# Sample attention of a hybrid decoder step on Trainium2: two samples over two GLU units, in one PSUM bank

## The chip, the cores and the metric
One core of a Trainium2 chip (trn2) runs the program. The metric is the device time of one execution in microseconds (us); of several runs the median counts. Engines are called PE (TensorE, the matmuls), DVE (VectorE), ACT (ScalarE), POOL (GpSimd) and SP (SyncE, which issues most transfers).

## The reference, cut to what matters
One layer of a decoder serves 256 prompt tokens and 8 samples of 4 new tokens each (288 tokens in all). Each token gets 16 query heads on 4 key/value heads of 64 features. A sample token attends over its sample's 256 cached positions (two pages of 128, found through a page table) and the 4 new ones; the indexer's choice of keys enters as a mask.

```python
def _dsa_block(q, qi, wi, qpos, k, v, ki, kpos):
    ...
    s = jnp.einsum('btngd,btjnd->btngj', qg, k_g) * (D_HEAD ** -0.5)
    s = jnp.where(valid[:, :, None, None, :], s, -jnp.inf)
    p = jax.nn.softmax(s, axis=-1)
    o = jnp.einsum('btngj,btjnd->btngd', p, v_g)
    return o.reshape(b, t, ATTN_W).astype(q.dtype)
...
    y_a = attn @ w_attn_proj
    z = jax.nn.gelu(s5_y).astype(x.dtype)
    glu_a, glu_g = jnp.split(z @ w_glu, 2, axis=-1)
    y_b = glu_a * jax.nn.sigmoid(glu_g)
    merged = jax.nn.sigmoid(ga) * y_a + jax.nn.sigmoid(gb) * y_b
    x = x + merged @ w_out
```

## The kernel before, in words
The kernel runs the layer as a stream of weight chunks. A chunk is 4 k-tiles x 256 columns (128x1024 values, one of 4 slots). SP loads it into raw, ACT rounds it to whi (`hi`, L861 to 868), DVE makes the rest wlo = raw - whi (`lo`, L1215 to 1220), and PE multiplies it in `group` (L511 to 533): three matmuls per k-tile and column tile, L528, L529, L530, with 288 tokens moving. Each engine runs its own list of instructions in order; semaphores join them. The stages follow each other: input projections, 8 gate units with the S5 scan, 8 GLU units (`N_GLU`), 4 projection units, w_out, w_up, w_down.

The change is in the 8 GLU units, 0 to 7. Each has two groups of two chunks (the gate columns into banks 2 and 3 of acc, then the value columns into banks 0 and 1), 96 big matmuls in all. The attention is laid between them: unit i does pair of prompt heads i and sample i.

- **PE** (L680 to 779). `unit_head`, before the first group: prompt values of unit i-1 (L724), prompt scores of unit i (L687), transposes of the sample's probabilities (L538 on psb). `unit_middle`, before the second group: sample values (L739 on the two pages, L741 on the four new keys), prompt transposes (L538 on ps), scores of sample i+1 (L696). Unit 0 is irregular: the scores of sample 0 are in its head, its transposes in the middle, and its values and the scores of sample 1 ahead of the second chunk of the second group (`first_samples`).
- The scores of one sample: for each pair p of key/value heads, qbs (128 feature rows of two heads x 32 columns, 16 per head, zeros for the other head) are the weights and the 260 keys move; the output is 32 partitions x 260 in bank 3 of aux. The values: vpg (128 positions x 64 features) are the weights, and 16 columns of probabilities pTb move; the output is already turned (features on partitions), in bank 0 of aux. A matmul of fp32 operands shows as two records.
- **DVE** (L1525 to 1600) masks and takes the maximum, scales psb by the reciprocal of the sum before it is transposed, and makes att_lo. **ACT** (L1048 to 1115) does the exponentials, the copies to pTs and pTb, att_hi, and the Sigmoid of the gate half (L1112), which frees the gate banks for the next unit. The exponential and the Sigmoid need different function tables; each switch loads one.
- **POOL** (L1950 to 2015) copies queries and new keys into qs, ks, qbs and kTb with a multiplication by `half` (1 for one half of the rows and 0 for the other) or by ones, then starts the transfers of the gates (gbt, ga) and multiplies yb. **SP** (L441 to 474) loads the next chunk of w_glu, the pages of the sample (`pages_in`) and its mask in between.
- Early in the program DVE builds small constants (`constants`, L1307 to 1317) after its tiles of the keys' chunks; the next thing that it does is the wlo of the values' first chunk (L1220). POOL fills `half` (L1763 to 1765) at its start, ahead of the S5 angles (L1768, L1771), whose sine ACT takes at L954 and L955.

Of the kernel before, what the change touches and what calls it, by code (L numbers as in the profile page):

```python
# [108 lines left out]
def hybrid_decoder_step_kernel(nc, I, O, W):  # L109
# [72 lines left out]
    half = at("half", [P, 2], F32, GR + 36832)  # L182
# [40 lines left out]
    qbs = at("qbs", [P, NPR, 32], F32, WK + 43168)  # L223
    psb = at("psb", [64, SK], F32, WK + 16160)
    pTb = at("pTb", [P, 3, 64], F32, WK + 17216)
    smax = at("smax", [64, 8], F32, WK + 18016)
# [6 lines left out]
    spare = at("spare", [P, 8], F32, WK + 43424)  # L233
    maskb = [at(f"maskb{i}", [64, SK], F32, GR + 10240 + 1056 * i) for i in range(2)]
# [26 lines left out]
    with ExitStack() as ctx:  # L261
# [22 lines left out]
        def sample_half(n):  # L284

            return aux[DH * n:DH * (n + 1), 0, 3 * P:3 * P + 64].rearrange("p (a n g t) -> p a n g t", a=2, n=2, g=4)[:, :, n, :, :]

        def sample_cols(tile, rows, b):

            return tile[rows, :, ds(TP + DS * b, DS)].rearrange("p (a g) t -> p a g t", a=2)  # L290
# [27 lines left out]
        def _(sp):  # L318
# [122 lines left out]
            def pages_in(i):  # L441

                u = i % 2
                pages = [sp.value_load(ptab[0:1, NPAGES * i + g:NPAGES * i + g + 1], min_val=0, max_val=NPOOL - 1) for g in range(NPAGES)]
                sp.wait_ge(sem("unit_free"), i + 1)
                for g, page in enumerate(pages):
                    sp.dma_start(kTb[u][:, :, P * g:P * (g + 1)], I["cache_k"][ds(page, 1)].rearrange("a (p q) s -> q (a p) s", p=NPR)
                                 ).then_inc(sem(f"k_in{u}"), 16)
                sp.dma_start(vnew[u][:, :], W["v_new"][DS * i:DS * (i + 1), :]).then_inc(sem(f"v_in{u}"), 16)
                for g, page in enumerate(pages):  # L450
                    sp.dma_start(vpg[u][:, g:g + 1, :], I["cache_v"][ds(page, 1)].rearrange("a p d -> p a d")).then_inc(sem(f"v_in{u}"), 16)

            def mask_in(i):

                sp.wait_ge(sem("mask_out"), 16)
                sp.dma_start(maskb[i % 2][:, :], bc(W["mask"][DS * i:DS * (i + 1), :], 0, 16)).then_inc(sem(f"mask_in{i % 2}"), 16)

            sp.wait_ge(sem("vs_stored"), 16)
            for i in range(N_GLU):
                load("w_glu", C_GLU + 4 * i, 0, 0, D + CW * i)  # L460
                pages_in(i)
                if i:
                    mask_in(i)
                load("w_glu", C_GLU + 4 * i, 1, KCH, D + CW * i)
                for q in range(2):
                    load("w_glu", C_GLU + 4 * i, 2 + q, KCH * q, CW * i)
                if i == 0:
                    mask_in(i)
# [30 lines left out]
        def _(pe):  # L499
# [190 lines left out]
            def sample_scores(i):  # L690

                u = i % 2
                pe.wait_ge(sem(f"k_in{u}"), 32 * (i // 2) + 32)
                pe.wait_ge(sem("new_ready"), 3 * i + 3)
                for p in range(NPR):
                    mm = pe.matmul(aux[32 * p:32 * p + 32, 3, 0:SK], qbs[:, p, :], kTb[u][:, p, :], start=True, stop=True)  # L696
                mm.then_inc(sem("ss_t"), 1)
# [9 lines left out]
            def sample_probs(i):  # L707
# [19 lines left out]
            def sample_values(i):  # L727

                u = i % 2
                pe.wait_ge(sem("pTb_ready"), i + 1)  # L730
                pe.wait_ge(sem(f"v_in{u}"), 48 * (i // 2) + 48)
                for p in range(NPR):
                    for g in range(NPAGES + 1):
                        for n in range(2):
                            c = slice(P * p + DH * n, P * p + DH * (n + 1))
                            k = slice(32 * p + 16 * n, 32 * p + 16 * (n + 1))
                            o = aux[DH * n:DH * (n + 1), 0, 3 * P + 32 * p + 16 * n:3 * P + 32 * p + 16 * (n + 1)]
                            if g < NPAGES:
                                mm = pe.matmul(o, vpg[u][:, g, c], pTb[:, g, k], start=g == 0, stop=False)  # L739
                            else:  # L740
                                mm = pe.matmul(o, vnew[u][:, c], pTb[0:DS, 2, k], start=False, stop=True)  # L741
                mm.then_inc(sem("unit_free"), 1)
# [12 lines left out]

            def unit_middle(i):

                pe.wait_ge(sem("p_ready"), i + 1)
                if i:
                    sample_values(i)  # L760
                prompt_probs(i)
                if i == 0:
                    sample_probs(0)
                elif i < N_GLU - 1:
                    sample_scores(i + 1)

            def first_samples():

# [1356 lines left out]
```

## Time and profile before
| what | value |
|---|---|
| median of 3 runs | 1564.46 us (1564.35 to 1564.78) |
| the profiled execution's own time | 1563.48 us |
| its span | 1561.6 us, 34462 instructions |
| PE busy | 1548.6 us, 99% |
| DVE, ACT, POOL busy | 1034.7 (66%), 668.0 (43%), 463.5 (30%) us |
| granted PE clock | 1.0 of full speed |
| GLU stage in the trace | about 411.6 to 552 us |

The page lists busy times and idle times of every engine; idle time of an engine off the path costs nothing. The view of the chain that ended last gives pieces in order of time, each starting where the one before ended, so that their lengths add up. The timeline gives start and duration of instructions (matmuls overlap, so durations there are longer than their distance); what stands in brackets is the idle time before an instruction and what ended it.

### The profile page before, as it was taken

Reading aid. Unit: us, or ns where it says so; the run is one execution under the profiler, and the core shown is the slowest. Engines: PE = TensorE matmul, PEld = TensorE weight load, DVE = VectorE, ACT = ScalarE, POOL = GpSimd, SP = SyncE. Lnnn points to the kernel's source line nnn. Section 1 sums busy time; section 2 is a strip of 40 time slices with the busy share of each in tenths; the row PEclk is TensorE's granted clock in tenths of the full one; section 3 lists DMA queues with packets and bytes.
Section 4 is the critical chain, followed back from the end, with each engine's and each line's share of the span. In section 5 each row is a group of like instructions: output and inputs, shape, how many; then the busy total and the mean of one; then the engine's idle time right before and its main releaser. Section 6 shows DMA issues by size and latency. Waiting matters only on the chain.

```text
span 1561.6 us, 34462 instructions
## 1 busy us (share of the span) xinstructions
PE 1548.6 (99%) x12846; PEld 1529.0 (98%) x12846; DVE 1034.7 (66%) x1487; ACT 668.0 (43%) x899; POOL 463.5 (30%) x601
## 2 busy tenths in 40 slices
PE   9999999999999999999999999999999999999998
PEld 9999999999999999999999999999999999999998
DVE  7755788888566666557776777777767664444443
ACT  6334345445477644444333333333434333333332
POOL 8994467876232200221121211111111110000100
PEclk9999999999999999999999999999999999999999
DMA  8887476666666677556545454555555565555552
GB/s 268 237 180 204 144 207 188 187 194 177 213 190 186 189 178 228 168 168 205 185 148 186 149 181 154 175 159 163 161 161 163 160 216 176 173 170 174 169 180 89
DMA packets 292928, 281.17 MB, mean 180 GB/s; under 512 B 29872, under 2 KB 283568, under 8 KB 292704
## 3 DMA queue, kind: packets, MB, share of 16 engines
q1 hardware_dynamic: 277264, 255.94, 54.2%
q10 hardware_dynamic: 13568, 16.62, 3.5%
q0 software_dynamic: 2000, 7.27, 1.4%
q8 instruction: 68, 1.11, 0.3%
q14 instruction: 28, 0.23, 0.0%
HBM read 266.60 MB, written 13.16 MB: 179 GB/s over the span
## 4 chain that ended last, share of the span: by engine, by line
PE 92%; POOL 5%; issue 1%; DVE 1%; DMA 1%; ACT 0%; SPq 0%; POOLq 0%; ACTq 0%
PE banks L528 29%; PE banks L530 29%; PE banks L529 29%; POOL angle L1768 1%; POOL angle L1771 1%; PE banks L538 1%; POOL sm L1768 1%; DMA raw<-in_w_in 1%; PE banks L651 1%; PE banks L665 1%; POOL sm L1771 1%; PE banks L687 0%; PE banks L724 0%; PE banks L739 0%; POOL rdec L1771 0%
## 5 line engine op out<-in xcount | busy, mean ns | idle before, releaser
L1220 DVE TENSOR_TENSOR wlo<-raw,whi 128x1024 fp32r<-128x1024 f32 x443 | 564.9, 1289 | 279.7 <-ACT whi L868 273.5
L868 ACT ACTIVATE whi<-raw 128x1024 fp32r<-128x1024 f32 x443 | 461.6, 1050 | 544.5 <-PE banks L530 482.7
L529 PE MATMUL banks<-h_lo,whi 128*128 128x288 f32 x1408 | 415.7, 295 | 0.0
L530 PE MATMUL banks<-h_hi,wlo 128*128 128x288 f32 x1408 | 415.7, 295 | 0.0
L528 PE MATMUL banks<-h_hi,whi 128*128 128x288 f32 x1408 | 414.6, 294 | 0.0
L528 PE MATMUL banks<-hhi,whi 128*128 128x288 f32 (+1 forms) x912 | 272.2, 298 | 3.3 <-DVE wlo L1220 1.6
L529 PE MATMUL banks<-hlo,whi 128*128 128x288 f32 (+1 forms) x912 | 270.0, 296 | 0.0
L530 PE MATMUL banks<-hhi,wlo 128*128 128x288 f32 (+1 forms) x912 | 269.9, 296 | 0.0
L529 PEld LDWEIGHTS banks<-h_lo,whi 128*128 128x128 f32 x1408 | 264.6, 188 | 0.1
L530 PEld LDWEIGHTS banks<-h_hi,wlo 128*128 128x128 f32 x1408 | 264.4, 188 | 0.0
L528 PEld LDWEIGHTS banks<-h_hi,whi 128*128 128x128 f32 x1408 | 264.1, 188 | 0.1
L529 PE MATMUL banks<-a_lo,whi 128*128 128x288 f32 x704 | 208.0, 295 | 1.0 <-issue 1.0
L530 PE MATMUL banks<-a_hi,wlo 128*128 128x288 f32 x704 | 207.8, 295 | 0.0
L528 PE MATMUL banks<-a_hi,whi 128*128 128x288 f32 x704 | 207.2, 294 | 0.0
L528 PEld LDWEIGHTS banks<-hhi,whi 128*128 128x128 f32 (+1 forms) x912 | 171.4, 188 | 6.3 <-issue 2.5
L529 PEld LDWEIGHTS banks<-hlo,whi 128*128 128x128 f32 (+1 forms) x912 | 171.4, 188 | 0.1
L530 PEld LDWEIGHTS banks<-hhi,wlo 128*128 128x128 f32 (+1 forms) x912 | 171.4, 188 | 0.0
L529 PEld LDWEIGHTS banks<-a_lo,whi 128*128 128x128 f32 x704 | 132.3, 188 | 1.2 <-issue 1.2
L530 PEld LDWEIGHTS banks<-a_hi,wlo 128*128 128x128 f32 x704 | 132.2, 188 | 0.0
L528 PEld LDWEIGHTS banks<-a_hi,whi 128*128 128x128 f32 x704 | 132.1, 188 | 0.0
L2018 POOL TENSOR_TENSOR sq<-x 128x576 f32 (+1 forms) x15 | 17.2, 1147 | 352.3 <-DVE x L1706 222.0
L1742 POOL TENSOR_TENSOR up<-cstate,ones 128x16 f32<-128x16 f32 x88 | 72.5, 824 | 154.2 <-DVE wlo L1220 141.4
(332 smaller groups left out, 2208.1 us busy)
## 6 DMA issues: line engine op xcount, KB each, us to landing
raw<-in_w_up SPq DMA_DIRECT2D x352, 256.0 KB, 3.4
raw<-in_w_in SPq DMA_DIRECT2D x223, 256.0 KB, 3.4
raw<-in_w_down SPq DMA_DIRECT2D x176, 256.0 KB, 2.9
raw<-in_w_glu SPq DMA_DIRECT2D x64, 256.0 KB, 3.1
raw<-in_w_out SPq DMA_DIRECT2D x64, 256.0 KB, 3.3
raw<-in_w_attn_proj SPq DMA_DIRECT2D x32, 256.0 KB, 3.9
scratch_gates<-gt ACTq DMA_DIRECT2D x16, 288.0 KB, 3.8
gbt<-scratch_gates POOLq DMA_DIRECT2D x8, 288.0 KB, 3.3
```

The costliest lines, as they stand in the source:

```text
L528: pe.matmul(out, h, xh[:, kt, :], start=kt == 0, stop=False)
L529: pe.matmul(out, h, xl[:, kt, :], start=False, stop=False)
L530: mm = pe.matmul(out, lo, xh[:, kt, :], start=False, stop=kt == nk - 1)
L538: return pe.matmul(out, in_, ident[b:b + k, b:b + k], is_transpose=True)
L651: mm = pe.matmul(aux[r, c, NCH * i:NCH * (i + 1)], lbs[r, i, c, :], ub[r, it, i, :], start=True, stop=True)
L665: mm = pe.matmul(out, clam[jt % 2][:, i, step, b + 1, :], xs[:, step, i, :], start=step == 0, stop=False)
L868: act.activation(whi[:, s, :, 0:cols], raw[:, s, :, 0:cols], ACT.Copy).then_inc(hi_ready, 1)
L1220: dve.tensor_tensor(wlo[:, s, :, 0:cols], raw[:, s, :, 0:cols], whi[:, s, :, 0:cols], ALU.subtract).then_inc(lo_ready, 1)
L1742: return pool.tensor_tensor(out, a, one.broadcast_to(list(out.shape)), ALU.mult)
L1768: own.link(pool.tensor_scalar(out, a, s1, s2, o1, o2))
L1771: own.link(pool.tensor_tensor(out, a, b, op))
L2018: own.link(pool.tensor_tensor(buf[:, :, :], x[:, ds(tile, 2), :], x[:, ds(tile, 2), :], ALU.mult))
```

## The change
Samples are taken in pairs j (samples 2j and 2j+1) over units 2j and 2j+1. Scores of both samples in the head of the even unit: 8 matmuls over one half of the rows each (64 feature rows of one head), 32 columns of weights, 260 keys moving, output to four strips of 32 partitions of bank 3, so that the 128 rows hold 4 heads x 4 queries per head x 2 samples x 4 tokens; the columns of the other sample are zeros in qbs, and the second sample accumulates on the first. One maximum and one exponential serve 128 rows. The probabilities are transposed unscaled in the middle of the even unit (three transposes of 128 rows; in unit 0 ahead of the second chunk of the second group). In the head of the odd unit they are the weights (32 columns) and the values move (64 columns), into four strips of bank 3: 24 matmuls. DVE scales these rows and puts each sample's part in place (`sample_rows`), and PE turns the 128x128 tile o_rows once in the middle of the odd unit. Nothing of the samples is in bank 0 any more. DVE gets two small constants, e8 and of_pair; POOL loses `half` and gets one memset of qbs.

```diff
@@ SP @@
+            def keys_in(j):
+                sp.wait_ge(sem("ss_t"), j) if j else sp.wait_ge(sem("pages_free"), 1)
+                for b in range(2):
+                    for g, page in enumerate(pages(2 * j + b)):
+                        sp.dma_start(kTb[b][:, :, P * g:P * (g + 1)], I["cache_k"][ds(page, 1)]
...
+            def values_in(j):
+                if j:
+                    sp.wait_ge(sem("sv_ready"), j)
+                for b in range(2):
+                    i = 2 * j + b
+                    sp.dma_start(vnew[b][:, :], W["v_new"][DS * i:DS * (i + 1), :]).then_inc(sem("v_in"), 16)
+                    for g, page in enumerate(pages(i)):
+                        sp.dma_start(vpg[b][:, g:g + 1, :], I["cache_v"][ds(page, 1)].rearrange("a p d -> p a d")).then_inc(sem("v_in"), 16)
...
                 load("w_glu", C_GLU + 4 * i, 0, 0, D + CW * i)
-                pages_in(i)
-                if i:
-                    mask_in(i)
+                if i == 0:
+                    keys_in(0)
                 load("w_glu", C_GLU + 4 * i, 1, KCH, D + CW * i)
+                if i % 2 == 0:
+                    values_in(j)
+                elif j < 3:
+                    keys_in(j + 1)
+                    mask_in(j + 1)
@@ PE @@
+            def sample_scores(j):
+                pe.wait_ge(sem("k_in"), 64 * j + 64)
+                pe.wait_ge(sem("new_ready"), 4 * j + 4)
+                if j:
+                    pe.wait_ge(sem("atts_done"), j)
+                for b in range(2):
+                    for p in range(NPR):
+                        for n in range(2):
+                            r, h = slice(DH * n, DH * (n + 1)), 2 * p + n
+                            mm = pe.matmul(aux[32 * h:32 * h + 32, 3, 0:SK], qbs[r, p, b, :], kTb[b][r, p, :], start=b == 0, stop=b == 1)
...
-                pe.wait_ge(sem("sp_ready"), i + 1)
+                pe.wait_ge(sem("sexp_ready"), j + 1)
                 for m, n in ((0, P), (1, P), (2, DS)):
-                    t = transpose(aux[0:n, 3, 64 * m:64 * (m + 1)], psb[:, m * P:m * P + n])
+                    t = transpose(aux[0:n, 3, P * m:P * (m + 1)], psb[:, m * P:m * P + n])
...
+            def sample_values(j):
+                pe.wait_ge(sem("pTb_ready"), j + 1)
+                pe.wait_ge(sem("v_in"), 96 * j + 96)
+                for b in range(2):
                     for g in range(NPAGES + 1):
+                        for h in range(NKV):
+                            k, c = slice(32 * h, 32 * (h + 1)), slice(DH * h, DH * (h + 1))
+                            o = aux[k, 3, DH * b:DH * (b + 1)]
                             if g < NPAGES:
+                                mm = pe.matmul(o, pTb[:, g, k], vpg[b][:, g, c], start=g == 0, stop=False)
                             else:
+                                mm = pe.matmul(o, pTb[0:DS, 2, k], vnew[b][:, c], start=False, stop=True)
+                mm.then_inc(sem("sv_ready"), 1)
+            def sample_turn(j):
+                pe.wait_ge(sem("o_rows_ready"), j + 1)
+                transpose(aux[:, 3, 0:P], o_rows[:, :, :].rearrange("p a d -> p (a d)")).then_inc(sem("so_t"), 1)
             def unit_head(i):
                 if i:
                     prompt_values(i - 1)
-                    pe.wait_ge(sem("atts_done"), i)
                 prompt_scores(i)
-                if i:
-                    sample_probs(i)
+                if i % 2 == 0:
+                    sample_scores(i // 2)
                 else:
-                    sample_scores(0)
+                    sample_values(i // 2)
             def unit_middle(i):
                 pe.wait_ge(sem("p_ready"), i + 1)
-                if i:
-                    sample_values(i)
                 prompt_probs(i)
...
+                if i % 2:
+                    sample_turn(i // 2)
+                elif i:
+                    sample_probs(i // 2)
@@ ACT @@
                 hi(c, 2)
                 prompt_exp(i)
-                if i == 0:
-                    sample_exp(0)
                 hi(c, 3)
+                if i % 2 == 0:
+                    sample_exp(i // 2)
                 prompt_probs_t(i)
...
+                if i % 2:
+                    sample_out(i // 2)
+                elif i:
+                    sample_probs_t(i // 2)
                 hi(c, 4)
                 if i == 0:
-                    sample_out(0)
-                if i < N_GLU - 1:
-                    sample_exp(i + 1)
+                    sample_probs_t(0)
@@ DVE @@
                 own.link(dve.tensor_reduce(e32[:, :], ident[:, :].rearrange("p (a h) -> p h a", a=4), AX_X, ALU.add))
+                own(dve.tensor_reduce(e8[:, :], ident[:, :].rearrange("p (x y) -> p y x", y=8), AX_X, ALU.add))
                 dve.tensor_tensor(ddiag[:, :, :], bc(e32[:, :], 1, NUT), bc(nvec[:, 48:56], 2, 32), ALU.mult).then_inc(sem("ddiag_ready"), 1)
+                own.wait()
+                own(dve.tensor_reduce(of_pair[:, :], e8[:, :].rearrange("p (b t) -> p b t", b=2), AX_X, ALU.add))
...
-                dve.tensor_scalar(psb[:, :], psb[:, :], smax[:, 2:3], None, ALU.mult).then_inc(sem("sp_ready"), 1)
+                own.link(dve.tensor_scalar(smax[:, 3:5], of_pair[:, :], smax[:, 2:3], None, ALU.mult))
+            def sample_rows(j):
+                dve.wait_ge(sem("sv_ready"), j + 1)
+                own.link(dve.tensor_scalar(o_rows[:, :, :], bc(aux[:, 3, 0:DH], 1, 2), smax[:, 3:4], None, ALU.mult))
+                dve.scalar_tensor_tensor(o_rows[:, :, :], bc(aux[:, 3, DH:2 * DH], 1, 2), smax[:, 4:5], o_rows[:, :, :], ALU.mult, ALU.add
+                                         ).then_inc(sem("o_rows_ready"), 1)
...
                 prompt_scale(i)
-                if i == 0:
-                    sample_scale(0)
+                if i % 2 == 0:
+                    sample_max(i // 2)
+                else:
+                    sample_rows(i // 2)
                 lo(c, 3)
...
+                if i % 2 == 0:
+                    sample_scale(i // 2)
+                else:
+                    sample_low(i // 2)
                 lo(c, 4)
@@ POOL @@
-            own.link(pool.memset(half[:, :], 0.0))
-            for n in range(2):
-                own.link(pool.memset(half[DH * n:DH * (n + 1), n:n + 1], 1.0))
...
-                if i < N_GLU - 2:
-                    pool.wait_ge(sem("ss_t"), i + 2)
-                    stage_sample(i + 2)
+                if i % 2 == 0 and i < N_GLU - 2:
+                    pool.wait_ge(sem("ss_t"), i // 2 + 1)
+                    stage_sample(i // 2 + 1)
                 gate_branch(i)
```

## Rows read from the trace of the kernel before

**Rows 1.** The page: busy time of the engines, and the group of ACT's rounding.
```profile
PE 1548.6 (99%) x12846; PEld 1529.0 (98%) x12846; DVE 1034.7 (66%) x1487; ACT 668.0 (43%) x899; POOL 463.5 (30%) x601
...
L868 ACT ACTIVATE whi<-raw 128x1024 fp32r<-128x1024 f32 x443 | 461.6, 1050 | 544.5 <-PE banks L530 482.7
```

**Rows 2.** Waits of PE over the span (us in total, times, longest).
```profile
PE banks L724 <- ACT glu_gate L1112: 0.7, 1, 0.7
```

**Rows 3.** Chain of waits, unit 4 of the GLU stage: start us, us, what.
```profile
482.39 0.81 PE banks L724 x12
483.19 0.86 PE banks L687 x8
484.06 0.16 PE banks L538 x3
...
490.79 0.34 PE banks L739 x8
491.13 0.22 PE banks L741 x4
...
491.91 0.81 PE banks L538 x6
492.71 0.56 PE banks L696 x4
493.28 0.33 PE banks L528
```

**Rows 4.** Chain of waits, middle of unit 0 and of unit 7.
```profile
419.87 0.98 PE banks L538 x9
...
544.29 0.80 PE banks L538 x6
545.09 0.13 PE banks L528
```

**Rows 5.** Chain of waits, other stages: indexer (L627), S5 inputs (L651), output transposes.
```profile
154.61 1.01 PE banks L627 x16
...
179.31 1.15 PE banks L651 x32
...
1550.40 3.21 PE banks L538 x28
```

**Rows 6.** Timeline of PE, S5 outputs: start us, us, engine line op names shapes.
```profile
401.19 0.43 PE L665 MATMUL banks<-xs,clam 128*32 128x72 f32 x16
401.44 0.31 PE L667 MATMUL banks<-ub,tlag 128*32 128x72 f32 x8
401.56 0.43 PE L665 MATMUL banks<-xs,clam 128*32 128x72 f32 x16
```

**Rows 7.** Timeline of ACT, end of unit 0.
```profile
427.33 0.51 ACT L1078 ACTIVATE psb<-psb,smax 64x260 f32<-64x260 f32 x1 [1.54 <-DVE smax L1548]
...
427.95 1.28 ACT L1112 ACT_TABLE_LOAD   x1
429.24 0.65 ACT L1112 ACTIVATE glu_gate<-banks 128x576 f32<-128x576 f32 x1
```

**Rows 8.** Timelines of POOL, ACT, DVE and PE around the constants.
```profile
5.67 0.10 POOL L1763 MEMSET half<- 128x2 f32 x1
...
6.16 0.56 POOL L1771 TENSOR_TENSOR sm<-params 128x32 f32<-128x32 f32 x2
...
82.42 0.74 ACT L954 ACTIVATE angle<-angle 128x640 f32<-128x640 f32 x1 [5.56 <-POOL angle L1826]
...
104.69 0.37 DVE L1316 TENSOR_REDUCE e<-ident 128x32 f32<-128x128 f32 x1
...
107.62 0.37 PE L528 MATMUL banks<-hhi,whi 128*128 128x288 f32 x1 [1.55 <-DVE wlo L1220]
```

**Rows 9.** Timelines of DVE and POOL in unit 4.
```profile
489.34 0.69 DVE L1540 TENSOR_TENSOR ps<-ps,pmax 128x512 f32<-128x512 f32 x1
...
493.37 0.44 POOL L1742 TENSOR_TENSOR qbs<-qT,half 128x32 f32<-128x32 f32 x2 [6.56 <-PE banks L696]
```

More of the change, by code:

```diff
@@ L181, in hybrid_decoder_step_kernel @@
     wtok = at("wtok", [P, 2, IH], F32, GR + 36608)
-    half = at("half", [P, 2], F32, GR + 36832)
+    e8 = at("e8", [P, 8], F32, GR + 36800)
+    of_pair = at("of_pair", [P, 2], F32, GR + 36832)
     nramp = at("nramp", [P, 32], F32, GR + 36672)
@@ L222, in hybrid_decoder_step_kernel @@
     kTb = [at(f"kTb{i}", [P, NPR, SK], F32, (WK + 41088, GR)[i]) for i in range(2)]
[L223 to L226, printed above, removed]
+    qbs = at("qbs", [P, NPR, 2, 32], F32, WK + 43168)
+    psb = at("psb", [P, SK], F32, WK + 16160)
+    pTb = at("pTb", [P, 3, P], F32, WK + 17216)
+    smax = at("smax", [P, 8], F32, WK + 18752)
+    o_rows = at("o_rows", [P, 2, DH], F32, WK + 18784)
     glu_a = at("glu_a", [P, 2, T], F32, WK + 19456)
@@ L232, in hybrid_decoder_step_kernel @@
     vnew = [at(f"vnew{i}", [DS, KV], F32, GR + 8192 + 1024 * i) for i in range(2)]
-    spare = at("spare", [P, 8], F32, WK + 43424)
-    maskb = [at(f"maskb{i}", [64, SK], F32, GR + 10240 + 1056 * i) for i in range(2)]
+    spare = at("spare", [P, 8], F32, WK + 43680)
+    maskb = [at(f"maskb{i}", [P, SK], F32, GR + 10240 + 1056 * i) for i in range(2)]
     ga = at("ga", [P, KD, T], F32, GR + 12416)
@@ L439, in _ @@
                         lags_in(it)
[L441 to L451, printed above, removed]
@@ L453, in mask_in, with pages @@
-            def mask_in(i):
+            def pages(i):
+                return [sp.value_load(ptab[0:1, NPAGES * i + g:NPAGES * i + g + 1], min_val=0, max_val=NPOOL - 1) for g in range(NPAGES)]
+            def keys_in(j):
+                sp.wait_ge(sem("ss_t"), j) if j else sp.wait_ge(sem("pages_free"), 1)
+                for b in range(2):
+                    for g, page in enumerate(pages(2 * j + b)):
+                        sp.dma_start(kTb[b][:, :, P * g:P * (g + 1)], I["cache_k"][ds(page, 1)].rearrange("a (p q) s -> q (a p) s", p=NPR)
+                                     ).then_inc(sem("k_in"), 16)
@@ L467, in _ @@
                 if i == 0:
-                    mask_in(i)
+                    mask_in(0)
             with loop("SP", 0, N_PROJ) as it:
@@ L1035, in gates @@
                     act.wait_ge(sem("c_ready"), 4 * N_GATE)
-                    for k in range(2):
-                        act.activation(spare[:, k:k + 1], ident[:, 0:1], ACT.Copy).then_inc(sem("unit_free"), 1)
+                    act.activation(spare[:, 0:1], ident[:, 0:1], ACT.Copy).then_inc(sem("pages_free"), 1)
                 hi(c, 6)
@@ L1972, in _ @@
                     stage_prompt(0)
+                    own.link(pool.memset(qbs[:, :, :, :], 0.0))
                     stage_sample(0)
@@ L1977, in _ @@
                 turn_forward(it)
+            new_keys(1)
             pool.wait_ge(sem("last_ready"), 2 * N_GATE)
```

111 lines of the change are left out of this document (36 added, 75 removed).

## The prediction
> **What bounds the kernel now.** I read the page first: TensorE (PE) is busy 99% of the span, and ScalarE's rounding of the weights (L868) sat idle 544.5 us, 482.7 of them waiting for PE to give a weight slot back [rows 1]. The suppliers wait for PE, so what counts is time on PE's own queue, wherever it is saved. PE's waits behind the start of the program are then few: 0.7 us behind glu_gate [rows 2] and 1.55 us behind one wlo tile [rows 8]. So the question is how many microseconds of PE's queue the sample attention takes before and after, and whether a new wait appears.
>
> **How the queue is read.** The chain of waits runs along PE through the GLU stage, and its pieces lie end to end, so their lengths add. A unit has a head and a middle. Head of unit 4 (units count from 0): prompt values 0.81, prompt scores 0.86, sample transposes 0.16, first projection matmul 0.33. Middle: 0.34 + 0.22 for one pair of heads of the sample values (the next pair repeats it), prompt transposes 0.81, sample scores 0.56, first projection matmul 0.33 [rows 3]. A projection matmul costs 0.13 where the array's shape does not change before it (the piece at 545.09) [rows 4], so entering another shape adds 0.20 there. Head before: 0.81 + 0.86 + 0.16 + 0.33 = 2.16. Middle before: 2 x 0.56 + 0.81 + 0.56 + 0.33 = 2.82.
>
> **Price of the new steps.**
> - *Sample scores of two samples (S).* Eight matmuls of 64 rows x 32 columns x 260, two records each, over four column tiles. The indexer has the same 16 records of the same shape: 1.01 us, L627 [rows 5]. There all four used one row half; here two row halves write one bank. L651 does that for two tiles: 32 records of 72 columns in 1.15 us, 0.036 a record [rows 5]. Since 72 columns in steps of four tiles take 24 records in 401.56 - 401.19 = 0.37, thus 0.062 a step [rows 6], one after another L651's 32 would need 1.98. So halves do run side by side. I take S = 1.01. Bounds: below, 0.97 (four steps of 260 columns scaled from 0.062 x 260/72 = 0.22, and 0.09 for the change of shape, half of the 0.20 above); above, halves one after the other, four steps more, 1.01 + 4 x 0.22 = 1.89.
> - *Sample values of two samples (V).* Four column tiles, 64 columns moving. A step of four tiles costs 64/72 x 0.062 = 0.055. Per sample: 4 steps on pages, 2 on the new keys (4 rows), so two entries into another shape. What an entry costs I take from S: 1.01 - 4 x 0.22 = 0.13. V = 2 x (6 x 0.055 + 2 x 0.13) = 1.18; taken 1.20. Bounds: today a pair of heads takes 0.56 for six steps and two entries [rows 3]; with steps of at least 0.055 an entry is at most 0.115, giving V = 1.12 below. Above, 12 steps of 0.062 and four entries of 0.15: 1.34; with tiles two by two instead of four, 12 steps more, 1.86.
> - *Transposes.* 28 of 128 columns take 3.21, so 0.11 each [rows 5]. In unit 0, where they follow projection matmuls of the same shape, no entry is paid. After the change nothing of another shape stands before the prompt transposes in any unit, nor after them: the sample transposes are now 128 rows too. Six cost 0.66 against 0.81, and the next projection matmul 0.13 against 0.33.
>
> **Sum on PE.** Odd unit, after: head 0.81 + 0.86 + V 1.20 + 0.33 = 3.20; middle 6 + 1 transposes 0.77 + 0.13 = 0.90. Even unit from 2 on: head 0.81 + 0.86 + S 1.01 + 0.33 = 3.01; middle 9 transposes 0.99 + 0.13 = 1.12. A pair of units: 8.23 against 2 x (2.16 + 2.82) = 9.96, minus 1.73; three pairs (units 1 to 6): **-5.19**. Unit 7: before 2.16 + 1.12 + 0.80 + 0.13 = 4.21 [rows 4], after 3.20 + 0.90 = 4.10: **-0.11**. Unit 0: before, in pieces of the lengths of rows 3, 0.86 + 0.56 + 0.33 in the head and 1.12 + 0.56 + 0.33 ahead of the second half of its second group, and 0.98 + 0.33 in the middle [rows 4], in all 5.07; after 0.86 + 1.01 + 0.33, 0.66 + 0.13, 0.33 + 0.13, in all 3.45: **-1.62**. Together -6.9.
>
> **Waits.** The 0.7 us behind glu_gate comes from unit 0, where ScalarE waits 1.54 us for VectorE's smax of sample 1 before its Sigmoid [rows 7]; that sample is gone from unit 0. ScalarE now waits there for the sample transposes instead. Behind them PE has 24 matmuls of the half group, 3.1 us, before it wants the bank; two copies (at most 0.5), the table load 1.28 and the Sigmoid 0.65 [rows 7] take 2.4. I count **-0.7**, with 0 as the other bound.
> VectorE's constants gain two reductions, and they stand right before the wlo tile that PE waits 1.55 us for: this cost is exposed. The nearest reduction (e from ident) took 0.37 [rows 8]; I take 0.25 for one whose result is not waited for, and 0.1 for a tiny second one: **+0.35** (bounds 0.2 and 0.6). Three GpSimd memsets go, between 5.67 and 6.16, at the head of GpSimd's angle chain; ScalarE waited 5.56 us for its end, and the slots behind it feed that same wlo tile [rows 8]. A weight transfer lies between, so I take half: **-0.25** (bounds 0 and -0.5).
>
> **Costs counted at nothing, and their cover.** VectorE's two new row operations stand between prompt_scale and the next wlo tile, and PE waits for them at the turn. Today the scale ends at 489.34 + 0.69 = 490.03 [rows 9] and PE's middle follows at 490.79 [rows 3]: 0.76 spare. The longer odd head pushes PE 1.04 back from the same scores, the six transposes come first (0.66): 2.5 us of cover for at most 0.9 (two operations of at most 0.45). GpSimd's staging of the next samples moves up from 493.37, where it waited for PE [rows 9], to the scores in the even head, and the gbt and ga transfers behind it move up with it, about 6 us; they are read a unit's end later. SP's key loads wait for the scores of the even head, its value loads for sv_ready in the odd head; queued behind each are weight loads 2 and 3, which must wait for VectorE's third wlo tile of the unit anyway, later than both. The first keys are 4 transfers instead of 2 and the first values 6 instead of 3, issued about 0.45 us each before loads whose slots are not free.
>
> **Sum.** -6.9 - 0.7 + 0.35 - 0.25 = -7.5. Against the profiled execution's own 1563.48 (span 1561.6): 1556.0. That execution lies 1.0 under the median 1564.46, so for a median I say 1564.46 - 7.5 = **1557.0 us**.
>
> **Rivals.**
> - *A, row halves exclude each other in one bank.* S 1.89: +0.88 x 4 = 3.5, so 1560.5. Against it: L651, which does this for two tiles; for it: four tiles with mixed halves stand in no row. The Trainium skill, "TensorEngine Tiling (Array Packing)", section "Restrictions and Gotchas", speaks against the change here: different row tiles cannot use the same PSUM bank at once. By that sentence the sum would be this rival's; L651's 0.036 a record disagrees with it. 0.08.
> - *B, a wait takes the place of the removed ones* (glu_gate in unit 0 still late, or the turned rows late by 0.5 us in four odd units): 1557.7 to 1559. Inside the range; 0.08.
> - *C, slower: the four column tiles of one bank do not overlap at all.* S: 16 records x 0.22 + 0.13 = 3.65, V: 48 x 0.055 + 4 x 0.13 = 3.16. Over four sample pairs +2.64 x 4 + 1.96 x 4 = 18.4: 1575.4. It ends slower than before once 7.5/18.4 = 41% of the overlap is lost. Against: L627 and L665 write four tiles of one bank. 0.03.
> - *D, no net gain*: the weight stream behind cannot come earlier, or less than 3.1 us of the 7.5 arrives. For: nothing in rows 1; ScalarE waits for PE, not for weights. 1563. 0.06.
>
> **Chances.** Forecast 0.75, A 0.08, B 0.08, C 0.03, D 0.06. A measurement of this kernel can tell about 0.2% (3.1 us) from no change; forecast, A and nearly all of B lie beyond it: faster 0.90, same 0.07, slower 0.03. Range: bottom, V 1.12 (-0.3), GpSimd's full 0.5 (-0.25), constants 0.2 (-0.15), some 0.6 between executions: 1555.7. Top, A: 1560.5.
>
> **What would show it.** In the changed kernel's chain: S as one piece of 16 records and 1.01, V in pieces of 48 records and about 1.2, first projection matmul of every middle 0.13, no idle before the prompt values of unit 1, PE's wait behind wlo near 107 us at 1.5 to 1.9. Odd head plus middle 4.1, even 4.13. I am wrong if S is near 1.9, if PE idles at a turn for o_rows, or if GLU shortens by 7 while the end does not.

## The result, and the profile after

The changed kernel takes 1552.88 us (median of 4 runs, 1552.31 to 1553.59); the kernel before took 1564.62 beside it (4 runs, 1564.35 to 1565.62). The ratio is 0.9924, 95% interval 0.9907 to 0.9941: 11.7 us less, where 7.5 were forecast, so the time lies below the range. Two more sets of the same kernel gave 1554.57 (ratio 0.9934 [0.9918, 0.9951]) and 1554.59 (0.9934 [0.9920, 0.9948]): 10 us less. The profiled execution took 1552.46 (span 1550.6), 11.0 less than the one before.

The page of the changed kernel, its PE row and ScalarE's rounding group, which answer to [rows 1]: PE is still full, ScalarE still waits for PE.

```profile
PE 1539.1 (99%) x12870; PEld 1522.0 (98%) x12870; DVE 1032.7 (67%) x1469; ACT 664.1 (43%) x874; POOL 463.4 (30%) x591
...
L882 ACT ACTIVATE whi<-raw 128x1024 fp32r<-128x1024 f32 x443 | 461.6, 1050 | 540.5 <-PE banks L546 492.3
```

The chain of waits of the changed kernel (start us, us, what), which answers to [rows 3, 4]: unit 0, the odd unit 1, the head of unit 2, and the middle of unit 5 (six prompt transposes and the turn). L703 and L744 are the prompt's scores and values, L716 the samples' scores, L757 and L759 their values on the pages and on the new keys, L554 transposes, L544 to L546 projection matmuls.

```profile
409.76 0.86 PE banks L703 x8
410.62 1.01 PE banks L716 x16
411.63 0.33 PE banks L544
...
418.21 0.66 PE banks L554 x6
...
422.05 0.33 PE banks L554 x3
...
425.55 0.81 PE banks L744 x12
426.36 0.86 PE banks L703 x8
427.22 0.36 PE banks L757 x16
427.58 0.24 PE banks L759 x8
427.82 0.36 PE banks L757 x16
428.19 0.24 PE banks L759 x8
428.43 0.33 PE banks L544
...
434.99 0.76 PE banks L554 x7
...
443.79 1.01 PE banks L716 x16
...
501.36 0.76 PE banks L554 x7
502.12 0.13 PE banks L544
```

The reader is to see three things. S is one piece of 1.01, as taken. V is 0.36 + 0.24 + 0.36 + 0.24 = 1.20, as taken. And the first projection matmul of the middle, now right behind the transposes, is 0.13, where it was 0.33 behind the sample scores in [rows 3]. From the first prompt scores (409.76) to the last prompt values (piece of 0.81 at 541.66) the stage takes 131.90; in the trace of before the same two pieces lie 411.88 and 551.46 apart, so 139.58. The stage is **7.68 us shorter**.

PE's waits in the two kernels (us in total, times, longest). Of before:

```profile
PE banks L528 <- DVE wlo L1220: 1.6, 1, 1.6
...
PE banks L529 <- issue: 1.0, 1, 1.0
```

and of after, the whole list:

```profile
PE banks L544 <- DVE hlo L1256: 3.0, 3, 1.6
PE banks L565 <- POOL ident L1760: 1.6, 1, 1.6
PE banks L544 <- DVE uq L1295: 0.3, 1, 0.3
```

The wait behind glu_gate [rows 2] is gone, and so are two others: the one behind wlo [rows 8], and an idle microsecond that the profile lays to "issue", which means that PE waited for nothing that the profile shows. What is left lies in the first 69 us of the program. The idle microsecond, called the stall from here on, stands in before at the first matmuls of w_down, in PE's timeline:

```profile
1268.30 0.40 PE L529 MATMUL banks<-a_lo,whi 128*128 128x288 f32 x1 [1.00 <-issue]
```

ScalarE at the end of unit 0 of the changed kernel (timeline; in brackets the idle time before and what ended it), to be held against [rows 7]:

```profile
422.41 0.38 ACT L1101 ACTIVATE pTb<-banks 128x256 f32<-128x256 f32 x1 [1.75 <-PE banks L554]
422.69 0.25 ACT L1102 ACTIVATE pTb<-banks 4x128 f32<-4x128 f32 x1
422.96 1.28 ACT L1122 ACT_TABLE_LOAD   x1
424.25 0.65 ACT L1122 ACTIVATE glu_gate<-banks 128x576 f32<-128x576 f32 x1
```

The Sigmoid ends at 424.9, and PE begins its next piece, the head of unit 1, at 425.55 without having waited: 0.6 us to spare. VectorE in the odd unit 5 (timeline):

```profile
498.38 0.68 DVE L1553 TENSOR_TENSOR ps<-ps,pmax 128x512 f32<-128x512 f32 x1
499.10 0.35 DVE L1572 TENSOR_SCALAR o_rows<-banks,smax 128x128 f32<-128x128 f32 x1
499.48 0.35 DVE L1573 SCALAR_TENSOR_TENSOR o_rows<-banks,smax,o_rows 128x128 f32<-128x128 f32 x1
```

The rows are in place at 499.83; PE turns them last of the seven transposes that begin at 501.36, so at about 502.0: 2.2 us of cover, against the 2.5 less 0.9 of the forecast.

**Where the 11.0 us came from.** Take the n-th large matmul (288 columns moving) in both traces and see how much earlier it starts in the changed kernel. The first one is 0.26 us ahead; the lead grows by 0.05 up to 80 us, by 1.78 around 107 us (the idle 1.55 of the wlo wait, and slower first matmuls behind it), by 7.68 in the GLU stage, by 1.27 at the first matmuls of w_down, and by 0.02 elsewhere: 11.06 in all at the last one.

### The profile page after: what moved, and what is told of

The parts are those of the page before. It is cut to its first block, busy times and chain, and to the rows that moved or that the text cites. A ratio compares the mean times of both kernels' runs of the same rounds, so it can differ in the third digit from the quotient of the medians.

```text
span 1550.6 us, 34501 instructions
## 1 busy us (share of the span) xinstructions
PE 1539.1 (99%) x12870; PEld 1522.0 (98%) x12870; DVE 1032.7 (67%) x1469; ACT 664.1 (43%) x874; POOL 463.4 (30%) x591
## 3 DMA queue, kind: packets, MB, share of 16 engines
q8 instruction: 68, 1.11, 0.3%
## 4 chain that ended last, share of the span: by engine, by line
PE 98%; DMA 0%; DVE 0%; SPq 0%; ACT 0%; ACTq 0%; issue 0%
PE banks L544 31%; PE banks L546 31%; PE banks L545 31%; PE banks L554 1%; PE banks L667 1%; PE banks L681 1%; PE banks L703 0%; PE banks L744 0%; DMA raw<-in_w_in 0%; PE banks L716 0%; PE banks L599 0%; PE banks L683 0%; PE banks L626 0%; PE banks L757 0%; ACT whi L882 0%; DVE wlo L1230 0%
## 5 line engine op out<-in xcount | busy, mean ns | idle before, releaser
L546 PE MATMUL banks<-h_hi,wlo 128*128 128x288 f32 x1408 | 416.3, 296 | 0.0
L544 PE MATMUL banks<-h_hi,whi 128*128 128x288 f32 x1408 | 415.2, 295 | 0.0
L544 PE MATMUL banks<-hhi,whi 128*128 128x288 f32 (+1 forms) x912 | 271.7, 298 | 3.4 <-DVE hlo L1256 3.0
L546 PE MATMUL banks<-hhi,wlo 128*128 128x288 f32 (+1 forms) x912 | 269.4, 295 | 0.0
L546 PEld LDWEIGHTS banks<-h_hi,wlo 128*128 128x128 f32 x1408 | 264.7, 188 | 0.0
L544 PEld LDWEIGHTS banks<-h_hi,whi 128*128 128x128 f32 x1408 | 264.4, 188 | 0.1
L546 PE MATMUL banks<-a_hi,wlo 128*128 128x288 f32 x704 | 208.1, 296 | 0.0
L544 PE MATMUL banks<-a_hi,whi 128*128 128x288 f32 x704 | 207.5, 295 | 0.0
L544 PEld LDWEIGHTS banks<-hhi,whi 128*128 128x128 f32 (+1 forms) x912 | 170.6, 187 | 6.2 <-DVE wlo L1230 2.2
L546 PEld LDWEIGHTS banks<-hhi,wlo 128*128 128x128 f32 (+1 forms) x912 | 170.7, 187 | 0.0
L546 PEld LDWEIGHTS banks<-a_hi,wlo 128*128 128x128 f32 x704 | 132.3, 188 | 0.0
L544 PEld LDWEIGHTS banks<-a_hi,whi 128*128 128x128 f32 x704 | 132.2, 188 | 0.0
```

What stands on the lines that cost most here:

```text
L544: pe.matmul(out, h, xh[:, kt, :], start=kt == 0, stop=False)
L546: mm = pe.matmul(out, lo, xh[:, kt, :], start=False, stop=kt == nk - 1)
```

## The experiments

Two accounts stood against each other for the surplus of 3 to 4 us. *P, the change itself*: the three memsets gone from GpSimd's head bring the angles and the wlo tile forward, and that wait goes. *L, the layout of the program*: the change lengthens PE's list, and something in the supply of instructions goes with it. A third was left, *E*: executions of one kernel differ anyway at the wlo wait. In the sets below, before ran at 1564.36 (25 runs, the first four experiments), 1564.66 (13 runs, the fifth to the eighth) and 1564.49 (9 runs, the last four).

**1. The three memsets moved off GpSimd's head, in the kernel before.**

```diff
-            own.link(pool.memset(half[:, :], 0.0))
-            for n in range(2):
-                own.link(pool.memset(half[DH * n:DH * (n + 1), n:n + 1], 1.0))
...
             pool.tensor_scalar(a3, a3, -PI_IN, PI_IN, ALU.max, ALU.min).then_inc(sem("angles_ready"), 1)
+            own.link(pool.memset(half[:, :], 0.0))
+            for n in range(2):
+                own.link(pool.memset(half[DH * n:DH * (n + 1), n:n + 1], 1.0))
```

> The kernel before, with GpSimd's three memsets of half moved from the head of its angle chain to behind its end; nothing else. Theory P (the start of GpSimd's chain decides when the sines come, and with them the weight slots): the chain starts 0.3 to 0.5 us earlier, PE's wait of 1.55 us near 107 us shrinks by that or vanishes, time 0.3 to 1.8 us below the kernel before (ratio 0.9988 to 0.9998). Rival R (the wait near 107 us depends on something else of the change or on the execution): wait still 1.2 to 1.8, time within 0.3 us of the kernel before. In both, PE's stall of 1.0 us at the first w_down matmuls (near 1268 us) is still there, because PE's instructions are the same.

Measured: 1563.71 (10 runs), ratio 0.9998 [0.9988, 1.0007]. The sine came at 84.93, later than the 82.42 of [rows 8], and the waits behind wlo and glu_gate and the stall all stayed. PE's waits:

```profile
PE banks L528 <- DVE wlo L1220: 1.6, 1, 1.6
PE banks L529 <- issue: 1.0, 1, 1.0
```

The trace shows why the memsets bring nothing. Without them the first multiplication of GpSimd's chain starts at 5.95 instead of 6.16 (it then waits for a transfer of parameters), and by the multiplication of angle at 60 us the lead is gone: 60.01 against 59.95. The ratio by itself does not separate the two accounts, since its interval takes in all of P's range; the trace speaks against P.

**2. The two constants added to the kernel before.**

```diff
                 own.link(dve.tensor_reduce(e32[:, :], ident[:, :].rearrange("p (a h) -> p h a", a=4), AX_X, ALU.add))
+                own(dve.tensor_reduce(e8[:, :], ident[:, :].rearrange("p (x y) -> p y x", y=8), AX_X, ALU.add))
...
+                own.wait()
+                own(dve.tensor_reduce(of_pair[:, :], e8[:, :].rearrange("p (b t) -> p b t", b=2), AX_X, ALU.add))
```

> The kernel before, with the two reductions of the change (e8, of_pair) put into VectorE's constants and not used. My prediction priced them at +0.35 us of PE's wait near 107 us: wait 1.9, time +0.35. Rival (hidden behind something that ends later): wait 1.55, time unchanged. The page of the changed kernel shows the reductions at 0.34 and 0.08 from start to start, with the ddiag product 0.3 shorter than before, so they may also cost about 0.1 in all.

Measured: 1563.80 (10 runs), ratio 0.9998 [0.9988, 1.0007]. In this trace (sine at 81.46) the wlo wait is not there although VectorE had more to do, and the stall, with PE's list as in before, was twice as long:

```profile
PE banks L531 <- issue: 2.0, 1, 2.0
```

The two reductions lengthen VectorE's work between the 128x32 reduction and the next wlo from 1.03 us (104.69 to 105.72 in before) to 1.18 (99.26 to 100.44), so by 0.15 and not 0.35, and in this execution nothing waits for it. The stall is an event whose length varies.

**3. 32 more instructions on PE, in the kernel before**, with no work worth the name.

```diff
+            for _ in range(8):
+                pe.matmul(aux[0:32, 0, 0:1], ident[:, 0:32], ident[:, 0:1], start=True, stop=True)
             group(0, 0, C_U, KD, hhi, hlo, by_tile=True)
```

> The kernel before, with eight more tiny matmuls (one column, into an unused place) behind the eight warm-up matmuls, so that every later instruction of PE lies further on in its program. Theory L (the 1.0 us stall of PE at the first w_down matmuls, near 1268 us, hangs on where PE's instructions lie and on nothing that the change means to do): the stall is gone or has another length, time 1.0 us lower but for 0 to 0.5 at the start. Rival (it belongs to the kernel before, by its transfers at that place): stall 1.0 as before, time 0 to 0.5 us above the kernel before.

Measured: 1561.79 (10 runs, 1560.32 to 1562.89), ratio 0.9984 [0.9974, 0.9993]. Adding instructions made the kernel 2.6 us faster, and the stall at w_down is gone. PE's one wait in the GLU stage stayed:

```profile
PE banks L726 <- ACT glu_gate L1114: 0.7, 1, 0.7
```

That is L. In the trace the missing stall is worth 1.26; the wlo wait is absent too (1.78), which is E, and the start is 0.7 slower. How the 2.6 of the medians divide is not shown. The changed kernel's 1552.9 to 1554.6 lie 7.2 to 8.9 us below this kernel, which is the forecast's own part.

**4. The memsets back at GpSimd's head, in the changed kernel.**

```diff
+            own.link(pool.memset(half[:, :], 0.0))
+            for n in range(2):
+                own.link(pool.memset(half[DH * n:DH * (n + 1), n:n + 1], 1.0))
+
             def ts(out, a, s1, s2, o1, o2):
```

> The changed kernel, with the three memsets put back at the head of GpSimd's angle chain, unused. Theory P: the sines come 0.3 to 0.5 us or more later and part of PE's wait near 107 us comes back, time 0.3 to 1.8 us above the changed kernel's 1552.9, so 1553.2 to 1554.7. Rival R: no wait there, time 1552.9 within 0.3. The GLU stage keeps its length (heads of the units as in the changed kernel: 1.01 for the scores, 1.2 for the values).

Measured: 1553.79 (4 runs), ratio 0.9938 [0.9921, 0.9955], which takes in 0.9924 and 0.9934, the ratios without them. The sine came at 84.42 and the wlo wait is there, this time at 88 us, in PE's timeline:

```profile
88.05 0.40 PE L545 MATMUL banks<-hhi,whi 128*128 128x288 f32 x1 [1.70 <-DVE wlo L1231]
```

Taken alone this is what P forecast, in the wait and in the time (1553.2 to 1554.7), and not what R did. But the unaltered changed kernel, with no memsets, has the same wait in its third trace (experiment 12) and took 1554.57 and 1554.59 in its other two sets, more than this one: the outcome does not need the memsets.

**5. The changed kernel again.**

> The changed kernel once more, to be timed beside the others on one chip. 1552 to 1554. In its trace the GLU stage must again be 7.7 us shorter than before, and there must be no stall at the first w_down matmuls. Theory C (the wait of 1.6 to 1.8 us in the first 110 us comes and goes by execution, with the time at which the sines come, 80 to 85 us): it may be there or not. Rival (the change removes it): it is not there.

Measured: 1554.57 (4 runs), ratio 0.9934 [0.9918, 0.9951]; the GLU stage to the hundredth as in the first trace, sine at 82.00, no wlo wait, no stall. The 1.9 us by which its profiled execution is longer lie before 16 us: a wait of 2.6 behind hlo where the first trace has 1.6, and 13 matmuls at 0.24 instead of 0.13 behind it, with a granted clock of 0.50 between 12.5 and 15.9 us.

**6. 224 more instructions on PE, in the changed kernel**, so that its place behind them is that of before plus 257. A place is the number of PE's instructions that ran ahead of a matmul, counted in the traces; 33 of the 257 are the change's own (48 more for matmuls and their weights, 15 fewer for semaphores). The 8 warm-up matmuls, whose results nothing reads, are replaced by 64 of one column.

```diff
-            for n in range(8):
-                pe.matmul(aux[:, 0, 0:P], ident[:, :], ident[:, :], start=True, stop=True)
+            for n in range(64):
+                pe.matmul(aux[0:32, 0, 0:1], ident[:, 0:32], ident[:, 0:1], start=True, stop=True)
```

> The changed kernel with the 8 warm-up matmuls replaced by 64 tiny ones (one column moving), which shifts all later instructions of PE. By count of the records the change lengthens PE's program ahead of w_down by 33 instructions, nearly what b_pad added (32); with 224 more the place is that of the kernel before plus 257. Theory L256 (instructions come in pieces of 16 KB, that is 256, so that the place counts modulo 256): the stall of 1 to 2 us at the first w_down matmuls comes back, time 1 to 2.6 above the changed kernel, but for up to 1 us at the start. Rival (another period or none): no stall there.

Measured: 1557.40 (4 runs, 1556.82 to 1557.56), ratio 0.9953 [0.9936, 0.9969]. The stall is back. Chain of waits:

```profile
1258.03 2.51 issue
1260.54 0.29 PE banks L544
...
1261.40 0.24 PE banks L546
1261.64 0.24 PE banks L544
```

Behind 2.51 us of nothing come 14 matmuls at 0.24 instead of 0.13; together the place costs 4.2 us. The slow ones are a matter of the clock. In the view of the stretch from 1261.3 to 1264.6, the number behind POOL is the granted clock, 0.50, thus the lower of the two levels (1.2 and not 2.4 GHz):

```profile
1261.30:1264.60 3.30, 3.30 (x16) 3.30 (x15) 2.10 (x6) 0.87 (x3) 0.00 (x0) 0.50 0.70 240
```

It fell behind 2.5 us in which PE did nothing; behind the stalls of 1.0, 1.8 and 2.0 us in the other traces it did not. The time is 2.8 above the changed kernel beside it (experiment 5), a little more than the 2.6 allowed.

**7. 256 more instructions on PE, in the kernel before** (the same edit with 72).

> The kernel before with the 8 warm-up matmuls replaced by 72 tiny ones: PE's later instructions lie 256 further. Theory L256: the stall at the first w_down matmuls is there as in the kernel before (1 to 2 us), time as the kernel before within 1. Rival: stall gone or of another length, time about that of b_pad, 2 to 3 below.

Measured: 1566.36 (10 runs, 1564.2 to 1567.49), ratio 1.0010 [1.0000, 1.0020], 1.7 above before where at most 1 was expected. The stall is there, and long:

```profile
PE banks L529 <- issue: 1.8, 1, 1.8
```

Counting PE's instructions ahead of w_down from the kernel before, the stall is there at 0 (three traces), +256 and +257, and not at +32 and +33 (the changed kernel); experiment 10 adds +161, without it. That is L: what decides is the place, not how many instructions were added.

**8. The new keys' rows padded with zeros to 128, in the changed kernel.** Value matmuls on 4 rows become matmuls on 128 rows, so that the array's shape does not change within V; the result stays.

```diff
-                                mm = pe.matmul(o, pTb[0:DS, 2, k], vnew[b][:, c], start=False, stop=True)
+                                mm = pe.matmul(o, pTb[:, 2, k], vnew[b][:, c], start=False, stop=True)
...
+                    for b in range(2):
+                        act.activation(vnew[b][:, :].rearrange("p (a c) -> p a c", a=2), bc(ident[:, :], 1, 2), ACT.Copy, scale=0.0
+                                       ).then_inc(sem("pages_free"), 1)
...
+                    if i == 0:
+                        own(act.activation(pTb[:, 2, :], ident[:, :], ACT.Copy, scale=0.0))
```

> The changed kernel with the four new keys of a sample padded by zero rows to 128 (the rows of vnew and of pTb behind the fourth are written zero once by ScalarE), so that the sample values keep one shape of the array. If a change of shape costs what I took, 0.13 each, V falls from 1.21 to about 0.8 (three of four entries gone), the GLU stage by 4 x 0.4 = 1.6, time 1.6 below the changed kernel. Rival (the 4-row matmuls are cheap because of their few rows, and 128 rows cost more per step): V stays at 1.2 or grows.

Measured: 1552.19 (4 runs, 1551.85 to 1553.94), ratio 0.9924 [0.9907, 0.9940]. Its chain has V between 461.33 and 462.14, 0.81 instead of 1.20:

```profile
461.33 0.36 PE banks L757 x16
...
461.80 0.22 PE banks L757 x16
...
462.14 0.33 PE banks L544
```

Three changes of shape gone from V save 0.39, 0.13 each: what the forecast took for one. The stage is shorter by 4 x 0.39 = 1.6. The median is 2.4 below the changed kernel beside it (experiment 5) and 0.7 below its first set, so 1.6 is not read from the times here; experiments 11 and 12 come back to it.

**9. The same matmuls, tile by tile, in the changed kernel.**

```diff
-                for b in range(2):
-                    for p in range(NPR):
-                        for n in range(2):
+                for p in range(NPR):
+                    for n in range(2):
+                        for b in range(2):
...
-                for b in range(2):
-                    for g in range(NPAGES + 1):
-                        for h in range(NKV):
+                for h in range(NKV):
+                    for b in range(2):
+                        for g in range(NPAGES + 1):
```

> The changed kernel with the same matmuls in another order: the scores' two samples innermost, so that two matmuls (four records) in a row go to one column tile before the next tile comes; the values' heads outermost, so that twelve records in a row go to one tile. Nothing is left out. Theory 'neighbours': PE takes its matmuls in order and one overlaps only with neighbours of other tiles. Scores then 13 steps of 0.22 and one change of shape of 0.13, so S = 3.0 against 1.01; values 45 steps of 0.055 and 16 changes of shape of 0.13 (the page rows and the four new rows now alternate in every tile), so V = 4.6 against 1.20; the GLU stage longer by 2.0 x 4 + 3.4 x 4 = 21, the time near 1574. Theory 'queue': PE fetches far enough ahead to start the next tile's matmuls meanwhile; S stays at 1.01 and V grows by the changes of shape alone (12 more of 0.13), to 2.8; the GLU stage longer by 6, the time near 1559.

Measured: 1567.54 (one run; before 1564.49 beside it, 1562.0 to 1567.29). Chain of waits, scores of samples 4 and 5, then the values of unit 3:

```profile
484.01 1.03 PE banks L716 x16
...
464.12 0.34 PE banks L757 x4
464.45 0.23 PE banks L759 x2
464.68 0.34 PE banks L757 x4
465.02 0.23 PE banks L759 x2
```

S stays (1.03), so "neighbours" falls: four records in a row for one tile do not keep the next tile's waiting. V is 4.5 (464.12 to 468.63), near the 4.6 of "neighbours" and far from the 2.8 of "queue"; of the times neither came out, since each account has one of the two numbers wrong. An account that fits both: a run of one shape holds one tile's records alone here, so that between two changes of shape nothing is left to overlap, and 48 steps of 0.055 and 16 changes of 0.115 make 4.48. By it what decides is that all four tiles are in use between two changes of shape. This is worked out afterwards and not tested: that four records in a row for one tile can be bridged and twelve cannot would give the same V, and the padded keys of experiment 8 in this order would tell the two apart. Of the 15 us lost to the trace of after, 4 x 3.3 are that; 1.5 are 14 slower matmuls, most at 0.24, from 505.56 on, behind the values of unit 5. The granted clock is 0.51 there (505.2 to 508.7), as behind the stall of experiment 6; it fell behind 4.5 us in which PE worked without a pause, but with one tile at a time. Behind the same values in units 1, 3 and 7 it did not fall; why only here stays open.

**10. The scores issued twice, in the changed kernel.**

```diff
-                for b in range(2):
+                for b in (0, 1, 0, 1):
```

> The changed kernel with the 8 matmuls of the samples' scores issued twice, the second time starting anew, so that the result stays. If the steps of four tiles are what the scores cost, S goes from 1.01 to 1.01 + 4 x 0.22 = 1.89 in four units, and the GLU stage is longer by 3.5, nowhere more, nowhere a new wait in that stage. If the head of the even unit had room (PE waits for something there that the pieces hide), less than 3.5. PE's list of instructions is longer by 64 or 128 ahead of the projections to w_down, so its place behind them moves as well: whether the stall ahead of the first w_down matmuls is there (1 to 2.5 in four earlier runs, none in the others) is open here, and the GLU stage alone is compared.

Measured: 1557.88 (one run); S in the chain:

```profile
412.75 1.89 PE banks L716 x32
```

From 411.89 to 547.29 the stage takes 135.40, 3.50 more than after: exactly 4 x 0.88. So PE has nothing to spare in the even heads. The stall at w_down is absent; a wlo wait of 1.7 is there.

**11 and 12. Experiment 8 and the changed kernel once more, side by side in 5 runs each.**

> The kernel with the four new keys' rows padded with zeros to 128, once more, in more runs. In the trace of its first run the GLU stage was 1.6 shorter than that of the changed kernel. If that is real in the time, the ratio to before is lower than that of the changed kernel beside it on the same chip by 0.001, so 1551.3 against 1552.9; if the padding (a wider copy on ScalarE and a longer memset) costs elsewhere, equal.

> The changed kernel once more, as the companion of the padded one. Both theories: 1552.3 to 1554.6, a ratio of 0.9925 to 0.9935, no stall ahead of the first w_down matmuls, S 1.01 and V 1.20. The wait of 1.6 near 87 or 107 us may be there or not: three of eight earlier traces have it.

Measured: padded 1552.23 (1551.19 to 1552.56), ratio 0.9920 [0.9906, 0.9935]; changed 1554.59 (1553.84 to 1554.88), ratio 0.9934 [0.9920, 0.9948]. The single runs of the two do not overlap, and the padded kernel is the fastest of all; in the traces its GLU stage takes 130.35 against 131.90. The intervals of the ratios to before still overlap, so 1.6 is what the traces bear out. The two profiled executions are 3.1 apart (1554.64 and 1551.52), and the other half of that is the wlo wait of 1.6, which the changed kernel's trace has here and the padded one's has not; what makes up the rest of the 2.4 between the medians is not shown.

## Why the prediction was right and wrong

**Right: the GLU stage.** PE's own queue with the glu_gate wait was to lose 6.9 + 0.7 = 7.6; it lost 7.68. S 1.01 and V 1.20 came as taken, and so did the transposes: six 0.66, seven 0.76 (0.77), nine 0.98 (0.99). The two new row operations took 0.73 of the 0.9 allowed and are covered, and no new wait stands in the stage.

**Rivals.** A falls: with both row halves writing one bank S stayed at 1.01, and doubling it added 0.88 and not more. The sentence of the Trainium skill, "TensorEngine Tiling (Array Packing)", section "Restrictions and Gotchas", that different row tiles cannot use the same PSUM bank at once, does not hold for these matmuls; as with L651 [rows 5], the measurement decides. B did not come: 0.6 and 2.2 us of cover were left. C falls as stated, since the four tiles overlap, though experiment 9 shows how the same matmuls in another order use up the whole gain (GLU stage 146.87 against 139.58 before), by V alone (3.16 forecast for no overlap at all, 4.5 with the added changes of shape). D falls: the 7.68 us saved in the stage reach the end, and more.

**Wrong: the step "PE's waits behind the start of the program are then few: 0.7 us behind glu_gate [rows 2] and 1.55 us behind one wlo tile [rows 8]".** The same list of PE's waits has a third, 1.0 us laid to issue, at the first matmuls of w_down, and the prediction left it out without a word. It went with the change because the change makes PE's list 33 instructions longer ahead of that place; 8 useless matmuls in the kernel before do the same (ratio 0.9984 [0.9974, 0.9993]). It is worth 1.27 in the profiled executions of before and after, 2.25 in that of experiment 2; in the medians of experiment 3 the difference is 2.6, with an interval of 1.1 to 4.1. With it the sum would have been 8.8 to 10.1 us, and the three sets of the changed kernel lie 11.7, 10.1 and 9.9 below their before.

**Wrong: "this cost is exposed" (+0.35) and the GpSimd term (-0.25).** Together they expected this wait to grow by 0.1; between the two profiled executions it went, which is 1.78 the other way, so 1.88. With 1.27 for the stall, 0.08 in the GLU stage and 0.3 at the start this makes the 3.5 by which the 11.0 of these two traces exceed the 7.5. The 1.27 came with the length that the change happens to have. The wait at the wlo tile belongs to the execution and not to the kernel: three traces of the same changed kernel have the sine at 80.21, 82.00 and 85.39, and only the last has the wait (1.57). Over all fourteen traces: with the sine at 84.4 or later (four traces) there is a wait of 1.6 to 1.7 behind a wlo tile at 88 to 89 us; at 82.4 to 83.1 (three) it stands at 107 to 108 us with 1.55 in before and 0.97 in experiment 8, and is absent in experiment 3; at 82.0 or earlier (seven) there is none. Moving three memsets by hand changed nothing that can be told apart from this. The lateness arises within GpSimd's chain: the multiplication of angle that starts at 66.03 and takes 1.56 us in after takes 4.34 in experiment 12 (from 68.50) and 4.36 in experiment 1 (from 68.05). In experiment 4, also late, it takes 2.46 and more is lost ahead of it. Why the chain is slower in some executions is open.

**Wrong: the range.** 0.6 us between executions was too little: the runs of before spread over 5.3 us (1562.0 to 1567.29), and the three medians of the changed kernel over 1.7.

**Open.** The first set's 11.7 against the 10 of the other two lies within their intervals, and no run settles it. What exactly the chip does at the stall was not tried beyond its place; the last section has what the traces show of it.

## What to carry to other kernels

Where one engine is full, the sum over its queue in pieces of the chain came out right to 0.1 us in 7.7; what has to be added is every line of that engine's list of waits, also one that the profile gives no cause for, with the question whether the change moves it. Of a wait near the start of the program, look at more than one execution before a term is hung on it. And between two changes of the array's shape keep all four column tiles at work (V 1.20 against 4.5); where a few rows of zeros avoid a change of shape, they pay 0.13 us a time.

## What the runs showed of the hardware that was not expected

- PE can stand idle for 1.0 to 2.5 us with nothing waited for, at a place fixed by how many instructions lie ahead of it: present at 0, +256 and +257, absent at +32, +33 and +161. At +257 it comes one matmul earlier than at 0 and +256.
- Instructions come by a queue of their own, in packets of 16 KB: 68 packets are 1.11 MB in before and after, and the kernels at +256 and +257 have one packet more, 69. In all five traces with the stall, 6 us that begin just ahead of it hold two such packets; the same stretch of each of the nine traces without it holds one. Before (1265 to 1271) and after (1255 to 1261):

```profile
q8 instruction: 2, 0.03, 2.4%
...
q8 instruction: 1, 0.02, 1.0%
```

  That PE waits for such a packet fits this and is argued, not shown; that the pattern repeats every 256 is no more than these places fit.
- The granted clock fell to 0.5 (the 1.2 GHz level), and projection matmuls came at 0.24 instead of 0.13, behind 2.5 us of idle PE (experiment 6), behind waits of 1.8 and 2.6 us near the start (experiments 2, 3 and 5), and once behind 4.5 us of matmuls on one tile at a time (experiment 9). It stayed at 1.0 behind a wait of 2.1 at the start of experiment 8 and behind the stall of 2.0 in experiment 2, so the length of the idle time alone does not decide.
- Matmuls of 64 rows on either half of the array, writing four column tiles of one bank, overlap as well as the indexer's, which use one half (16 records in 1.01 both), even with four records in a row for one tile (1.03).
- A change of the array's shape costs 0.115 to 0.13 us between tiled matmuls, from 128 rows to 4 or back (worked out from experiments 8 and 9).
- The end of GpSimd's first chain varies by 5 us between executions of the same kernel (sine at 80.21 to 85.39).
